# Two-layer encoder trunk: layer loops written out, six PSUM banks for the FFN chunks, another order at the start, in the gate loop and at the last gate tile

## The reference

```python
for i in range(DEPTH):                                   # DEPTH = 2
    x = x + 0.5 * swiglu(rmsnorm(x, norm_ff1[i]), ff1_w_gate[i], ff1_w_up[i], ff1_w_down[i])
    x = x + token_mixer(rmsnorm(x, norm_mix[i]), ...)    # attention with top-k keys + gated linear attention
    x = x + 0.5 * swiglu(rmsnorm(x, norm_ff2[i]), ff2_w_gate[i], ff2_w_up[i], ff2_w_down[i])
    g = jax.nn.sigmoid(rmsnorm(x, norm_ple[i]) @ ple_w_gate[i])
    x = x + g * (p[i] @ ple_w_proj[i])
return rmsnorm(x, norm_final)
```

## Time and profile before

| | |
|---|---|
| median of 3 runs | 1238.77 us (1238.06 to 1240.99) |
| the profiled execution | 1238.23 us |
| its span, first to last instruction | 1236.4 us |
| TensorE busy | 1194.5 us, 97% |
| VectorE busy | 810.2 us, 66% |
| ScalarE busy | 594.8 us, 48% |
| POOL busy | 125.6 us, 10% |
| moved from and to HBM | 218.80 MB, mean 177 GB/s |

### The profile page before, as it was taken

The page is one execution under the profiler, slowest core; times in us unless marked ns, Lnnn a source line. Parts: engine busy times, 40 slices in busy tenths (PEclk is TensorE's granted clock), DMA queues, the critical chain, the costliest instruction groups (busy, mean ns, idle before and its releaser), DMA issues. The chain is left out here.

```text
span 1236.4 us, 23621 instructions
## 1 busy us (share of the span) xinstructions
PE 1194.5 (97%) x10226; PEld 1163.4 (94%) x10226; DVE 810.2 (66%) x916; ACT 594.8 (48%) x667; POOL 125.6 (10%) x137
## 2 busy tenths in 40 slices
PE   5999999999989999999989999999999999999997
PEld 5999999998889999999989999999888999999996
DVE  5666655687868666655756665548787676666545
ACT  6444444555555544443544443446455455444443
POOL 2000001002511100001200000100034120000011
PEclk9999999999999999999989999999998999999998
DMA  8555555444425555555355555554533355555540
GB/s 273 192 202 192 187 202 178 164 176 165 138 103 191 192 193 186 202 194 188 132 198 184 201 201 181 199 182 149 207 132 116 129 179 195 190 204 190 186 171 35
DMA packets 33736, 218.80 MB, mean 177 GB/s; under 512 B 5312, under 2 KB 5728, under 8 KB 7648
## 3 DMA queue, kind: packets, MB, share of 16 engines
q1 hardware_dynamic: 33632, 217.27, 49.8%
HBM read 216.21 MB, written 1.05 MB: 176 GB/s over the span
## 5 line engine op out<-in xcount | busy, mean ns | idle before, releaser
L1095 DVE TENSOR_TENSOR w_lo<-raw,w_hi 128x2048 fp32r<-128x2048 f32 x202 | 462.5, 2293 | 252.7 <-ACT w_hi L745 252.4
L745 ACT ACTIVATE w_hi<-raw 128x2048 fp32r<-128x2048 f32 x202 | 387.1, 1917 | 417.3 <-PE psum L359 407.1
L357 PE MATMUL psum<-hA_hi,w_hi 128*128 128x256 f32 x1376 | 384.4, 279 | 0.9 <-DVE gates L1142 0.9
L358 PE MATMUL psum<-hA_hi,w_lo 128*128 128x256 f32 x1376 | 380.5, 277 | 0.0
L359 PE MATMUL psum<-hA_lo,w_hi 128*128 128x256 f32 x1376 | 380.4, 276 | 0.0
L357 PEld LDWEIGHTS psum<-hA_hi,w_hi 128*128 128x128 f32 x1376 | 258.7, 188 | 5.0 <-issue 2.9
L358 PEld LDWEIGHTS psum<-hA_hi,w_lo 128*128 128x128 f32 x1376 | 258.8, 188 | 0.2
L359 PEld LDWEIGHTS psum<-hA_lo,w_hi 128*128 128x128 f32 x1376 | 258.7, 188 | 0.0
L357 PE MATMUL psum<-hB_hi,w_hi 128*128 128x256 f32 x832 | 233.9, 281 | 17.8 <-DVE w_lo L1493 7.8
L358 PE MATMUL psum<-hB_hi,w_lo 128*128 128x256 f32 x832 | 231.9, 279 | 0.0
L359 PE MATMUL psum<-hB_lo,w_hi 128*128 128x256 f32 x832 | 231.8, 279 | 0.0
(11 more groups left out here) (172 smaller groups left out, 1229.2 us busy)
## 6 DMA issues: line engine op xcount, KB each, us to landing
raw<-in_weights SPq DMA_DIRECT2D x203, 1024.0 KB, 4.8
x<-in_x SPq DMA_DIRECT2D x4, 256.0 KB, 4.8
raw<-in_weights SPq DMA_DIRECT2D x4, 256.0 KB, 5.8
out<-gates SPq DMA_DIRECT2D x4, 256.0 KB, 2.4
relu<-in_p SPq DMA_DIRECT2D x2, 256.0 KB, 5.0
consts<-in_consts SPq DMA_DIRECT2D x1, 448.0 KB, 10.2
gnorm<-in_gla_norm SPq DMA_DIRECT2D x2, 64.0 KB, 5.6
consts<-in_consts SPq DMA_DIRECT2D x1, 64.0 KB, 6.0
```

Source lines behind the costliest of these rows:

```text
L357: pe.matmul(o, lh, rh, start=start, stop=False)
L358: pe.matmul(o, ll, rh, start=False, stop=False)
L745: act.activation(w_hi[:, s, :], raw[:, s, :], ACT.Copy).then_inc(hi_ready[s], 1)
L1095: dve.tensor_tensor(w_lo[:, s, :], raw[:, s, :], w_hi[:, s, :].bitcast(F32), ALU.subtract).then_inc(lo_ready[s], 1)
```

## The change

- All engines have both layers written out; no hardware loop is left.
- FFN: the first two chunks keep their bank pairs. From the third on, each chunk fills one bank, the banks rotating over 6, 7, 0, 1, 2, 3. The waits on `gate_scaled` and `up_scaled` move back accordingly. `token_sums` moves to the middle of the second chunk, `spread` ahead of the third.
- Start: ScalarE issues the four pieces of the first chunk; SP issues x, then chunks 1 and 2, then the constants. Chunk 1 of the first layer is split in four pieces, with one square between them.
- Gate loop: another order on TensorE, ScalarE and VectorE.
- The last gate tile's two columns have banks of their own (5 and 7), and the first is passed on when half the chunk is multiplied. The final squares have a buffer of their own.

```diff
+LAST_TILES = (5, 7)
+UP_BANKS = (6, 7, 0, 1, 2, 3)
...
-                sp.dma_start(raw[:, 0, piece(i)], a["weights"][0, :, piece(i)]).then_inc(piece_landed[i] if i < 3 else landed[0], 16)
-            sp.dma_start(ident, a["consts"][:, 0:P]).then_inc(const_landed, 16)
             chunk(0, 1)
             chunk(0, 2)
...
-                token_sums(L, k, 4)
-                s = operands(L, off + 1)
-                pairs(s, 2, h, 0, range(8))
-                spread(L, k, 4)
-                pairs(s, 2, h, 1, range(8)).then_inc(chunk_done[s], 1)
-                for g in range(1, N_FF):
...
+                s = turn(L, off + 1)[0] if L == 0 and f == 0 else operands(L, off + 1)
+                for m in range(4):
+                    if m == 2:
+                        token_sums(L, k, 4)
...
+                    for c in range(2):
+                        mm = pairs(s, 2, h, c, (2 * m, 2 * m + 1))
+                mm.then_inc(chunk_done[s], 1)
+                for q in range(2, 2 * N_FF):
+                    s = operands(L, off + q)
+                    if q in (4, 5):
+                        pe.wait_ge(gate_scaled, F + 1)
+                    elif q in (6, 7):
+                        pe.wait_ge(up_scaled, F + 1)
+                    elif q >= 8:
+                        pe.wait_ge(up_scaled if q % 2 else gate_scaled, F + q // 2 - 2)
+                    if q == 2:
+                        spread(L, k, 4)
+                    by_columns(s, bank[UP_BANKS[(q - 2) % 6]], h)
...
+                    level(j)
                     turn_prob(j)
-                    level(j)
...
-                    by_columns(s, bank[4 + i], hA)
+                    if i < 3:
+                        by_columns(s, bank[4 + i], hA)
+                    else:
+                        pe.wait_ge(pgate_scaled, L * 4 + 2)
+                        pairs(s, LAST_TILES[0], hA, 0, range(8)).then_inc(tile_ready, 1)
+                        pairs(s, LAST_TILES[1] - 1, hA, 1, range(8)).then_inc(chunk_done[s], 1)
...
-            with pe.Fori(0, L_N) as L:
+            for L in range(L_N):
...
                 for j in range(8):
                     chunk_products(L, MGA + j)
+                    if j == 7:
+                        take_prob(7)
+                    split(L, MGA + j + 3)
                     if j < 6:
...
-                    if j == 6:
-                        take_prob(6)
-                    split(L, MGA + j + 3)
...
-                    if j < 6:
+                    if j < 7:
                         take_prob(j)
-                take_prob(7)
...
+            for i in range(4):
+                act.dma_start(raw[:, 0, piece(i)], a["weights"][0, :, piece(i)]).then_inc(piece_landed[i] if i < 3 else landed[0], 16)
...
-                    if j < 5:
-                        dve.wait_ge(gla_exp, L * 9 + 4 + j)
-                        distance(4 << j, (2 << j) - 1)
-                    if j == 6:
-                        normalise(7)
...
-                    split(L, MGA + j + 3)
-                    if 0 < j < 6:
-                        normalise(j + 1)
                     if j < 7:
                         for hh in range(2):
...
+                    split(L, MGA + j + 3)
+                    if 0 < j < 7:
+                        normalise(j + 1)
+                    if j < 6:
+                        mask_logits(j + 2)
+                    if j < 5:
+                        dve.wait_ge(gla_exp, L * 9 + 4 + j)
+                        distance(4 << j, (2 << j) - 1)
                     if j in (2, 4, 6):
                         rest_oa(j // 2 - 1)
-                    if j < 6:
-                        mask_logits(j + 2)
```

More of the change, by code:

```diff
@@ L194, in hybrid_trunk @@
         piece_lo = sem("piece_lo")
+        next_hi = sem("next_hi")
+        next_lo = sem("next_lo")
         const_landed = sem("const_landed")
+        masks_landed = sem("masks_landed")
         gain_landed = sem("gain_landed")
@@ L303, in chunk @@
                 s, t = turn(L, n)
-                if not (isinstance(L, int) and L == 0 and n < SLOTS):
+                if L or n >= SLOTS:
                     sp.wait_ge(lo_ready[s], t - 1 + START)
@@ L718, in _ @@
             pe.wait_ge(sq_added, of_norm(L_N, 0, 3) + START)
[L719 to L725, removed]
+            for c in range(3):
+                if c:
+                    pe.wait_ge(last_squares, c)
+                for t in range(2):
+                    half = slice(t * P, (t + 1) * P)
+                    mm = pe.matmul(bank[4][:, T + t:T + t + 1], last_squared[:, c - 1, half] if c else total[:, half], ones[:, 0:1],
+                                   start=c == 0 and t == 0, stop=c == 2, skip_group_check=True)
             mm.then_inc(sums_done, 1)
@@ L1000, in _ @@
                     first_squares(m - 1)
-            first_squares(3)
-            split(0, 1)
+            act.wait_ge(landed[1], 16)
+            for i in range(4):
+                act.activation(w_hi[:, 1, piece(i)], raw[:, 1, piece(i)], ACT.Copy).then_inc(next_hi if i < 3 else hi_ready[1], 1)
+                if i == 0:
+                    first_squares(3)
             split(0, 2)
-            with act.Fori(0, L_N - 1) as L:
+            for L in range(L_N - 1):
                 layer(L, False)
@@ L1074, in layer @@
                 steps[0] = before
-            with pool.Fori(0, L_N - 1) as L:
+            for L in range(L_N - 1):
                 layer(L, False)
@@ L1132, in mean_square, with products @@
                                   ).then_inc(diag_done, 1)
+            def products(q):
+                return high(2 * q) if q < 2 else tiles(UP_BANKS[(q - 2) % 6])
             def ffn(L, off, f, k, h):
@@ L1141, in ffn @@
                     chunk_products(L, n)
-                    dve.tensor_tensor(gate_sum, high(0), both(rb), ALU.mult).then_inc(gate_scaled, 1)
+                    dve.tensor_tensor(gate_sum, products(2 * g), both(rb), ALU.mult).then_inc(gate_scaled, 1)
                     if g:
@@ L1145, in ffn @@
                     chunk_products(L, n + 1)
-                    dve.tensor_tensor(up_sum, high(2), both(rb), ALU.mult).then_inc(up_scaled, 1)
+                    dve.tensor_tensor(up_sum, products(2 * g + 1), both(rb), ALU.mult).then_inc(up_scaled, 1)
                     dve.wait_ge(up_scaled, F + g + 1)
@@ L1450, in embed @@
                         split(L, n + 3)
-                chunk_products(L, PGATE + 3)
                 for c in range(2):
[L1453 to L1456, removed]
+                    if c:
+                        chunk_products(L, PGATE + 3)
+                    else:
+                        dve.wait_ge(tile_ready, L + 1)
+                    dve.tensor_tensor(gate_sum[:, c, :], bank[LAST_TILES[c]][:, 0:T], rb[:, :], ALU.mult
+                                      ).then_inc(pgate_scaled if c else tile_scaled, 1)
+                    if c == 0 and not last:
+                        rest_pair(L, 4, 2, hB)
                     dve.wait_ge(pgate_tanh if c else tile_tanh, (L * 4 + 4) if c else (L + 1))
                     g = gate_act[:, c, :]
[L1459 to L1462, removed]
+                    step(L, dve.scalar_tensor_tensor(out=g, in0=g, scalar=1.0, in1=tiles(3)[:, c, :], op0=ALU.add, op1=ALU.mult))
                     xs = x[:, 6 + c, :]
@@ L1494, in _ @@
                                   ).then_inc(piece_lo if m < 3 else lo_ready[0], 1)
-            split(0, 1)
+            for i in range(4):
+                if i < 3:
+                    dve.wait_ge(next_hi, i + 1)
+                else:
+                    dve.wait_ge(hi_ready[1], 1)
+                dve.tensor_tensor(w_lo[:, 1, piece(i)], raw[:, 1, piece(i)], w_hi[:, 1, piece(i)].bitcast(F32), ALU.subtract
+                                  ).then_inc(next_lo if i < 3 else lo_ready[1], 1)
+            split(0, 2)
             dve.wait_ge(const_landed, 16)
             mean_square(0, 0, 4)
-            split(0, 2)
-            with dve.Fori(0, L_N - 1) as L:
+            for L in range(L_N - 1):
                 layer(L, False)
```

44 lines of the change are left out of this document (20 added, 24 removed).

## The result

The changed kernel takes 1224.64 us (median of 4 runs, 1224.51 to 1226.05), the kernel before 1239.88 (its three runs of above and a fourth): ratio 0.9878, 95% interval [0.9864, 0.9891]. It is faster, but 8.6 us slower than forecast and outside the range. Its span is 1222.7 us, 13.7 less than before, where the sum promised 22.4.

A forecast was written before the change was run, and what follows sets the result against it. TensorE, 97% busy, was taken to set the pace, so only its pauses could yield time. Terms 5.5 + 5.6 + 5.1 + 6.0 + 0.9 - 0.7 = 22.4 us gave 1215.8 (1216 by the median); range 1211.5 to 1222.

The forecast's parts named there:

- Gate loop: Each layer's mixer loop: the new order removes TensorE's pauses, gaining 5.6 us in layer 1 and 5.1 in layer 2.
- POOL's keys for the next level: Gate loop: POOL's products, begun 3.4 after the chunk's end and taking 2.7 to 3.5, delay TensorE 0 to 0.1 us.
- waits on `lev_ready` in odd iterations: Gate loop: named beforehand as a sign that the prediction is wrong; no size given.
- Rival B: Gate loop trades its pauses for new ones: 4 us less gain, about 1220 us; chance 0.14.
- low clock: Layer boundary: TensorE's lower clock after the 4.97 us pause, counted as 2.0 us on top.
- Start: Kernel start, up to the third chunk: earlier matmuls gain 5.5 us, bounds 3 and 7.
- The boundary: Between the two layers: third chunk's matmuls start earlier, gaining 6.0 us, bounds 4 and 7.5.
- FFN 2: Both FFN 2 starts: later token sums delay the third chunk's split, costing 0.35 us each.
- The wait on `rest_oa(3)`: Behind each gate loop: it stands behind a split on VectorE, so TensorE waits 1.2 us.
- The tail: Kernel end: column 0 squared and summed in advance gains 0.9 us, bounds 0 and 1.5.
- Rival C: TensorE's written-out program is fetched slower than it runs; 1245 us at 0.35 per packet; chance 0.03.
- A: Start and boundary keep most of their waits, with a larger FFN 2 cost: about 1222 us; chance 0.15.

The follow-up runs named there:

- combo_four: Changed kernel with gate-loop splits behind small steps, third FFN chunk's split before the mean square, last gate tile step by step, first chunk's pieces issued by SP: 1208.02 us.
- split_first: Changed kernel with VectorE's split of the third FFN chunk ahead of the mean square, at both FFN 2 starts and the layer boundary: 1224.14 us.
- split_tiny: Changed kernel with VectorE's split in the gate loop cut from 2048 columns to 64, order of instructions kept: 1214.10 us.

## Why the prediction was wrong, step by step

**Gate loop: the step that failed** is "POOL's keys for the next level begin 3.4 after the chunk's end and take 2.7 to 3.5, against 6.9 until TensorE wants them, so 0 to 0.1". Start and need were right, the length was not. I took it from rows in which POOL met only short VectorE work or the tail of a split, though the new order puts the products beside a whole split; they take 4.7. Among the signs of an error I had named "waits on `lev_ready` in odd iterations", and those are what came: six, 6.0 us in all. Two lesser errors lie on top. Rival B had the kind of this outcome, but its argument looked at VectorE's work against TensorE's, and at 4 us for both layers; it was 6.3. And low clock was booked only at the boundary: layer 2's pauses cost 9.3 us before, not 6.5, because after its 2.10 pause TensorE ran for 9 us at a clock of 0.63, the lower of its levels for most of the time. The same pause in layer 1 left the clock at 1.00 (345 to 350 us), so this part was luck: that gain came on top of forecast, and without it the shortfall would have been larger. In the changed kernel part of the loss is of the same kind: the loop's window shows 0.97, and layer 1 lies 6.1 us above the bare work, of which the pauses (1.16, 1.31, 0.80 and 1.02, each with 0.17) make 5.0.

**Start: a term mis-sized**, 3.6 instead of 5.5. "So I put the first matmul 0.4 later": it came 2.1 later. In the timeline of the changed kernel ScalarE's own issuing moved the end of its table load from 2.58 to 4.43, so that its first copy could begin at 4.65 at best, 1.0 later than before: 0.4 was too little for that alone. The copy then waits until 5.80 for the gains, which SP issued at 1.16 in both kernels; the first tile of x lands 4.7 us after its issue instead of 2.7. Of the kernels with two queues this trace is the extreme (4.0 to 4.7). In the nine that keep this start, itself among them, the third chunk starts at 24.3 to 25.9 (25.1 in the mean), in the two with one queue at 24.1 and 24.0. So the second queue costs about 1.1. The other 0.8 is in part my "POOL's third sum near 14.4": it ended at 15.37 in before already, and at 15.87 in combo_four, where it takes 1.07 us beside a piece of VectorE's split instead of 0.74. The Trainium skill's "DMA: Bandwidth & Descriptors", section "Issuing engines are not separate DMA queues", which I had weighed there, grants a second issuer no more than the issuing time; no gain came here. That the first landings also get 1 to 2 us later is for these traces to show.

**What was right.** The boundary: 6.1 for 6.0, a wait of 1.56 where I had 1.7, then 0.85 where I had 1.1, and a granted clock of 1.00 behind them (624 to 630 us). FFN 2: 0.41 and 0.38 for 0.35, on a split; that the order of split and sums decides it is what split_first shows, at a gain of 1.1. The wait on `rest_oa(3)`: 1.02 for 1.2. The tail: 0.8 for 0.9. Rival C, instruction fetch: the instruction queue moved 1.33 MB in 81 packets against the earlier trace rows, and 161 us pass without a pause. The loops' 6.3 us alone already reach the edge of the range, and the range had room for A or for B, not for the parts of both that came.

## What to carry over

Before you move VectorE's work and GpSimd's against each other, look what ran on the other engine in the rows that you price from: one form of instruction with several lengths (here 1.29, 1.77, 1.90) is a sign that they met. Where the new order lets two such instructions meet, add the whole length of the other's to the later one. Put long, deferrable instructions behind all short ones that another engine waits for, and do not cut them up to "share": pieces let the rival in between. Remove the pauses of a loop first and try the microsecond terms afterwards, since pauses that shift from run to run hide them.

## What the runs showed of the hardware

- A POOL product of 128x512 f32 takes 1.27 to 1.30 us undisturbed and 3.32 to 3.44 when it waits out a split of 2.28; the split takes 3.35 behind a running product, and four quarters of it in turn with POOL's work take 5.2 to 5.8. Short VectorE work does it too: a product took 1.77 beside a `dist` of 0.69.
- VectorE's normalising of 128x128 by a column (L1314, x2) took 2.34 us where it takes 0.48 undisturbed: at 303.99, begun while `klev` ran (to 305.02), its second half ended at 306.33, just behind `qlev` (306.25). It reads one tile and a column. In split_tiny, with no long split near, it still took 1.52 beside `qlev` (begun 302.86, against 302.99 to 304.29). That this is the same lock was not tried by itself.
- With transfers issued from two engines at once the first 256 KB landed after 4.0 to 4.7 us in ten kernels, with one queue after 2.7 to 3.0 in three.
- A pause of a microsecond or two costs TensorE's clock in one place and not in another. Windows as in the earlier trace rows, in the changed kernel behind the 1.31 pause, in before behind the 2.10 pause of layer 1 and of layer 2:

```profile
323.00:326.00 3.00, 2.74 (x26) 2.27 (x28) 2.93 (x6) 0.98 (x1) 1.68 (x3) 0.79 0.97 303
...
345.00:350.00 5.00, 4.97 (x56) 4.53 (x56) 3.38 (x9) 2.85 (x7) 1.41 (x2) 1.00 0.58 210
...
951.80:961.00 9.20, 9.13 (x65) 8.36 (x66) 4.90 (x10) 4.47 (x8) 1.42 (x2) 0.63 0.30 114
```

The 1.28 pause of the changed kernel's layer 2 (941.8 to 950) and those of 1.56 and 0.85 at the boundary left it at 1.00. Why the one and not the other is open.
